# Sixteen-word gaps ahead of the two halves of the experts' gathered tokens

## The reference, cut to what matters

```python
def moe_swiglu(h, router, w_gate, w_up, w_down):
    top_v, top_i = lax.top_k(logits, TOP_K)
    ...
    for e in range(N_EXPERTS):
        y_e = swiglu(t, w_gate[e], w_up[e], w_down[e])   # (silu(t @ gate) * (t @ up)) @ down
        out = out + gates[:, e:e + 1] * y_e
```

## The kernel before

| begins at | tensors |
|---|---|
| 0 | `mslot0` to `mslot2`, `mix_parts` (over them), `consts`, `res`, the used start in `mixer_lows`, `x_pair` (byte 212736) and its second half (220928) |
| 64 | `weights_hi`, `weights_lo` (from byte 134720 on, 8192 each), `x_parts`, `hidden_hi`, `hidden_lo`, `mslot3` and `mslot3_parts`, `xn_hi`, `xn_lo`, `xT`, `one_hot`, `scratch` and `scratch_parts` (134720) |

## Time and profile before

### The profile page before, as it was taken

One profiled execution on the slowest core, in us unless ns is written; L12 is line 12 of the kernel. 1 busy time (PEld: TensorE's weight loads), 2 busy tenths in 40 slices (PEclk: granted clock), 3 DMA queues, 4 the chain that ended last, 5 costly groups with the idle time before them and its releaser, 6 DMA issues.

```text
span 2403.7 us, 34175 instructions
## 1 busy us (share of the span) xinstructions
PE 2382.4 (99%) x12542; PEld 2017.0 (84%) x12542; DVE 1872.4 (78%) x1961; ACT 1438.0 (60%) x1474; POOL 14.2 (1%) x34
## 2 busy tenths in 40 slices
PE   8999999999999999999999999999999999999998
PEld 7788899888888888888888888888788888897887
DVE  7767786678888888888888898677966676688666
ACT  6645455567777777777777776555254454544444
POOL 1000000000000000000000010000000000000000
PEclk9999999999999999999999999999999999999999
DMA  8375143459999999999999996853355566533653
GB/s 301 116 251 177 68 147 130 146 207 376 380 377 348 374 379 378 348 377 377 377 348 373 381 395 246 278 177 123 132 193 175 194 227 230 176 126 123 200 191 125
DMA packets 315952, 603.73 MB, mean 251 GB/s; under 512 B 9120, under 2 KB 135200, under 8 KB 315552
## 3 DMA queue, kind: packets, MB, share of 16 engines
q1 hardware_dynamic: 314160, 592.70, 69.1%
q10 hardware_dynamic: 1136, 7.87, 0.8%
q0 software_dynamic: 576, 2.10, 0.2%
HBM read 597.91 MB, written 8.91 MB: 252 GB/s over the span
## 4 chain that ended last, share of the span: by engine, by line
PE 94%; DVE 2%; ACT 1%; DMA 1%; DVEq 1%; issue 0%; SPq 0%; ACTq 0%
PE bank L205 20%; PE bank L206 20%; PE bank L207 19%; PE bank L1218 17%; PE bank L1222 9%; PE bank L3513 1%; PE bank L2955 1%; PE bank L3440 1%; PE bank L2230 1%; PE bank L2240 1%; DMA mslot<-in_e_w_in 1%; PE bank L2930 1%; PE bank L1714 1%; PE bank L1058 0%; PE bank L2149 0%; PE bank L2249 0%
## 5 line engine op out<-in xcount | busy, mean ns | idle before, releaser
L3205 DVE TENSOR_TENSOR weights_lo<-mslot,weights_hi 128x2048 fp32r<-128x2048 f32 x336 | 767.5, 2291 | 117.5 <-ACT weights_hi L3098 116.5
L3098 ACT ACTIVATE weights_hi<-mslot 128x2048 fp32r<-128x2048 f32 x336 | 644.0, 1919 | 217.4 <-PE bank L207 214.2
L1370 DVE TENSOR_TENSOR weights_lo<-scratch,weights_hi 128x2048 fp32r<-128x2048 f32 x165 | 377.2, 2289 | 166.3 <-ACT weights_hi L1363 166.2
L1218 PE MATMUL bank<-x_parts,weights_hi 128*128 128x512 f32 x1760 | 441.2, 392 | 1.8 <-DVE x_parts L921 1.8
L1218 PEld LDWEIGHTS bank<-x_parts,weights_hi 128*128 128x128 f32 x1760 | 319.4, 189 | 63.8 <-DVE x_parts L921 2.4
L205 PE MATMUL bank<-weights_hi,x_pair 128*128 128x512 f32 x896 | 356.9, 398 | 0.2 <-issue 0.2
L206 PE MATMUL bank<-weights_lo,x_pair 128*128 128x512 f32 x896 | 351.4, 392 | 0.0
L207 PE MATMUL bank<-weights_hi,x_pair 128*128 128x512 f32 x896 | 349.9, 391 | 0.0
L1363 ACT ACTIVATE weights_hi<-scratch 128x2048 fp32r<-128x2048 f32 x165 | 315.3, 1914 | 49.3 <-PE bank L207 49.0
L205 PE MATMUL bank<-weights_hi,hidden_hi 128*128 128x512 f32 x808 | 315.9, 391 | 0.0
L206 PE MATMUL bank<-weights_lo,hidden_hi 128*128 128x512 f32 x808 | 315.2, 390 | 0.0
(11 more groups left out here) (561 smaller groups left out, 2735.0 us busy)
## 6 DMA issues: line engine op xcount, KB each, us to landing
mslot<-in_o_moe_w_gate SPq DMA_DIRECT2D x112, 1024.0 KB, 6.8
mslot<-in_o_moe_w_up SPq DMA_DIRECT2D x112, 1024.0 KB, 6.8
mslot<-in_o_moe_w_down SPq DMA_DIRECT2D x112, 1024.0 KB, 6.9
scratch<-in_ffn_w_gate SPq DMA_DIRECT2D x44, 1024.0 KB, 5.2
scratch<-in_ffn_w_up SPq DMA_DIRECT2D x44, 1024.0 KB, 5.1
scratch<-in_ffn_w_down SPq DMA_DIRECT2D x44, 1024.0 KB, 5.0
mslot<-in_o_w_in SPq DMA_DIRECT2D x7, 2048.0 KB, 10.8
scratch<-in_e_ffn_w_gate SPq DMA_DIRECT2D x11, 1024.0 KB, 5.2
```

Of the source, the lines that this page charges most:

```text
L1218: pe.matmul(m.ps[bank + j][:, :], hi[:, k, cols(j)], both, start=(k == 0), stop=False)
L1370: dve.tensor_tensor(m.wlo[to][:, :], m.fslot[i], m.whi[to][:, :], ALU.subtract).then_inc(m.sig["f_lo"], 1)
L3098: act.activation(m.whi[(place + half) % PLACES][:, :], r.slot[slot + half], ACT.Copy).then_inc(s["r_hi"], 1)
L3205: dve.tensor_tensor(m.wlo[i][:, :], r.slot[slot + half], m.whi[i][:, :], ALU.subtract).then_inc(s["r_lo"], 1)
```

## The change

A tensor `phase3` of 16 words (64 bytes) is placed ahead of `x_pair`, and `x_pair` gets 16 words more. Its first half (`xg[0]`, the high part) then begins at byte 212800, 64 modulo 128, and the second (`xg[1]`, the low part), with another gap of 16 words before it, at byte 221056, 0 modulo 128. `m.xg` is a list of two tiles in place of one tile with an axis of two. In `odd_out_piece` the high part of the first half of block 9 was a slice of `x_pair` at word 2000; it is now written as a slice of `scratch_parts` at word 21504, which is byte 220736 like the slice before.

```diff
--- before.py
+++ after.py
@@ -48,6 +48,8 @@
 NE, FE = 8, 3584
 FC = 512
 NC = FE // FC
+
+PHASE = 16
 
 DA, DB, DC = 384, 256, 384
 AT = DA // P
@@ -190,7 +192,9 @@
     with nc.sbuf_tensor("mixer_lows", [P, f0 + 3 * PIECE - 6 * PIECE - KT * 2 * SEQ - 2 * HALF], F32R) as lows:
         m.c_low = [cut(lows, f0 - 6 * PIECE - KT * 2 * SEQ - 2 * HALF + i * KT * DC, KT, DC) for i in range(2)]
     sb("scratch_rest", f0 + PIECE - 6 * PIECE - KT * 2 * SEQ - 2 * HALF)
-    m.xg = cut(sb("x_pair", 2 * PIECE, F32R), 0, 2, KT, 2 * P)
+    sb("phase3", PHASE)
+    xg = sb("x_pair", 2 * PIECE + PHASE, F32R)
+    m.xg = [cut(xg, i * (PIECE + PHASE), KT, 2 * P) for i in range(2)]
     return m
 
 
@@ -496,7 +500,7 @@
     ks = slice(half * KT // 2, (half + 1) * KT // 2)
     wide = lambda t: t.rearrange("p (k n) -> p k n", n=HALF)
     if b == 9:
-        hi = m.xg.rearrange("p i k t -> p (i k t)")[:, PIECE - 48:2 * PIECE - 48] if half == 0 else \
+        hi = m.scr_parts(21504, PIECE) if half == 0 else \
             m.x2.rearrange("p k i t -> p (k i t)")[:, 0:PIECE]
         low = m.b_low
     else:
@@ -2790,7 +2794,7 @@
     flat = lambda t: t.rearrange("p k t -> p (k t)")
     x2 = m.x2.rearrange("p k i t -> p (k i t)")
     r.yh, r.yl = (x2[:, (2 + i) * KT * P:(3 + i) * KT * P] for i in range(2))
-    r.xg = [m.xg[:, i] for i in range(2)]
+    r.xg = m.xg
     xT = flat(m.xT)
     r.silu, r.h = xT[:, 0:FC], xT[:, FC:2 * FC]
     r.oh = m.oh.rearrange("p (t s) -> p t s", t=NT)
```

## The result

| | before | after |
|---|---|---|
| median of 21 runs, us | 2406.18 | 2409.65 |
| lowest run, us | 2405.57 | 2409.23 |
| span of the profiled execution, us | 2403.7 | 2407.8 |

The ratio is 1.0015, with a 95% interval of 1.0008 to 1.0021: 3.5 us slower, certain in its sign and under the 0.2% (4.8 us) that the prediction took as its bound. The forecast was 2411.4. One of the 21 runs of after took 2962.15 us at a mean granted clock of 0.752; the ratio leaves it out.

What follows compares the result with a forecast made beforehand. PE's sequence of matmuls in the expert stage was taken as the bound. 896 triplets x 6.3 ns = +5.6 us on 2405.8 gave 2411.4 us; range 2400.8 to 2414.3, the likeliest case's own 2409.5 to 2414.3.

Steps and rivals of the forecast that it cites:

- What bounds the stage: In the experts, PE is busy 950.00 of 950 us, so the stage lasts as long as PE's own sequence of matmuls.
- No other cost: No instruction, wait or byte of traffic is added; only matmul spacing in the experts' gate and up products changes.
- 693.3 per triplet: Experts' gate and up: three matmuls (alike, alike, different in place from the weights) take 693.3 ns, against 687 before.
- a passage that never ends: On `x_pair`, each alike/different change costs some 27 ns over about five matmuls; triplets change again before three are done.
- The sum, 896 x 6.3 = 5.6 us: Experts' gate and up products: 896 triplets of three matmuls, each 6.3 ns longer, all on the path, +5.6 us.
- the mechanism's lower bound: Least slowdown from mixed places in the experts' triplets, 896 x 4.4 ns = +3.9 us; the upper bound was +8.3 us.
- 24 steps in 5.55 where now 5.50: Timeline sign on `x_pair` in the experts: 24 matmul steps take 5.55 us after, where 5.50 passes without waits before.
- 27 ns x 56: Products on `hidden` behind the up product: their passage cost of 27 ns, 56 times, stays, within 1.5 us either way.
- Modulo 128: Experts' matmuls: whether stationary and moving operand begin alike modulo 128 bytes sets the spacing, 226.5 ns alike, 229.0 different.
- rival 2: Experts' gate and up: the high half decides and PE falls into 226.7 ns steps, -6.3 us, 2399.5 us; chance 0.13.
- Rival 1: Experts' gate and up: each product has its own price, prices add to 682.3 ns per triplet, -4.2 us; chance 0.13.
- Rival 3: The change doesn't act; the spacing of `x_pair` comes from something else, time stays at 2405.8 us; chance 0.12.

Runs made afterwards that it cites:

- e4: Against after, same places, but each half of a gate or up product does eight products with the high half, then four with the low: 2410.59 us.
- e6: Against after, both halves of `x_pair` placed at 192 modulo 256 bytes, the weights being at 64: 2415.75 us.
- e1: Against after, the low half of `x_pair` also placed at 64 modulo 256 bytes, so both halves lie like the weights: 2401.39 us.
- e3: Against after, high half of `x_pair` back at 0 as in before, low half at 128 modulo 256 bytes: 2412.24 us.
- e8: Against after, high half of `x_pair` kept at 64, low half placed at 192 modulo 256 bytes: 2410.74 us.
- e12: Against after, both halves of `x_pair` placed at 48 modulo 256 bytes, 16 bytes below the weights: 2402.7 us.
- e5: Against after, both halves of `x_pair` placed at 128 modulo 256 bytes, 64 above the weights: 2415.78 us.
- e11: Against after, both halves of `x_pair` placed at 32 modulo 256 bytes, 32 below the weights: 2415.33 us.
- e2: Against after, the places of `x_pair` mirrored, high half at 0 and low half at 64 modulo 256 bytes: 2407.67 us.
- e9: Against after, both halves of `x_pair` at 64, and low weights of the FFN's gate and up products at 128 and 0 modulo 256: 2399.64 us.

## Why the prediction was right or wrong

- *What bounds the stage*: right. PE is busy throughout in both kernels. In the ten further kernels that move `x_pair` alone or reorder its products, the time moved by -4.6 to +9.6 us, and the 112 groups of 24 account for it to within 0.5 us, but for e4 and e6, where the groups on `hidden` add 1.1 and 1.5. DVE, ACT and DMA followed even e1's shorter stage.
- *No other cost; the difference wholly between 510 and 1465 us; `hidden` and the FFN unchanged*: right, to 0.1 us (970 to 974 us, 2734.7 to 2735.9 ns, 928.7 to 928.8 us).
- *693.3 per triplet*: the rows of two alike and one different were the right ones to take it from; that a value picked between 692 and 694 came out to 0.1 ns is luck. The reason, a passage that never ends, isn't borne out. What came is a settled repeat of three, of the very kind that the forecast said would not be there, and e4 gets the same sum with a quarter of the passages. The passage of some 27 ns exists (28 in e4), but four of them in twelve matmuls don't cost four times as much. "Medians over 392 in at least two lines" was wrong with it: one line is over (397), another is at 392.
- *The sum, 896 x 6.3 = 5.6 us*: this is the term that was mis-sized. It measured 3.6 us by the groups and 3.5 by the medians. That is under the +3.9 that the prediction gave as the mechanism's lower bound. It held a time over +0.2% (0.48) likelier than one between that and no change by this mechanism (0.14), and the less likely of the two came. The step that failed is to price all 896 triplets at the settled step and to let the edges stay. "24 steps in 5.55 where now 5.50" was +50 ns; the mean group gave +32. The forecast had a passage of five steps in its own rows, and a group has only 24, so the edges are a large part of it. Before pays 61 ns per group at its two edges, after 41. The exit was named as a cost that stays (27 ns x 56), but the entries, 112 of them, were not summed at all.
- *Modulo 128*: wrong, by e3 (+6.2 us, where nothing was to change) and e6 (+9.5, where it should have been as fast as e1). The rows of before could not show it. All of them with 512 columns lay at distances 0 and -64 modulo 256; the prediction's remark that the low half goes "to an odd line of 128" where "no row of before has a stationary operand" was the right doubt, weighed in rival 2 only.
- *Rival 1, each product has its own price*: in the forecast's form (a gain of 4.2 us) it is refuted by after itself. With the distance modulo 256 it is still refuted: after and e8 settle at 693.3 where prices would add up to 686.7.
- *Rival 2, the high half decides*: refuted by after. The rhythm that it promised exists, but only once the low half is alike too (e1).
- *Rival 3, no effect*: refuted: operands' places alone moved the kernel from 2401.4 to 2415.8 us. The rule of the Trainium skill cited in the prediction ("SBUF — State Buffer", section "Who interferes with whom") has two parts. That PE's two read ports are independent isn't borne out, if it means that the places of the two operands don't bear on each other: with a stationary operand at 64, the step is 226.7 ns with the moving one at 64 and 229.0 with it at 128. That PE never waits on anyone is said there of other engines, and no run here bears on that.

What stays open: why mixed places cost more than their parts (693.3 against 686.7), and why operands at the same places can keep either of two rhythms (e3, e6, e12). That the settled sums are 680, 686.7, 693.3 and 700, always 6.7 ns apart, but for 685 in e12 and 697.3 in e6, is a fact of the traces and not an explanation. Moving the weights instead of `x_pair` was not tried, nor distances under 16 bytes, nor whether places beyond 256 bytes count.

## What to carry to other kernels

Where PE is busy without a gap, read the distance from start to start in the timeline and compare it between products of one shape: if they differ, look at where stationary and moving operand begin, modulo 256 bytes at the least, and put both halves at the moving operand's place (here -4.6 us for a gap of 16 words; moving only the high half there cost +3.5). Price a rhythm over the mean group with its edges, not at the settled step, and don't take a period or a mechanism for settled when all rows at hand are two cases of it; one kernel with a shift of 128 bytes would have told. The place is to be tried, not reasoned: 16 bytes off cost 0.9 to 1.3 us, 32 bytes off some 13.5.

## What the runs showed of the hardware that was not expected

- Float32r matmuls of 512 columns with a weight load each, at full clock, start 226.7, 228.3, 229, 232.4 or 233.3 ns apart, by where the stationary operand lies against the moving one modulo 256 bytes; sign counts (-64: 229, +64: 233.3).
- They fall into repeats of between 2 and 12 matmuls (2 in e5, 3 in before and after, 4 in e11, 6 in e2, 7 in e6, 12 in e3 and e4) and stay there to the end of the group; what ran before a group goes with which repeat it takes (e3: 687 or 700 per triplet with operands at the same places).
- Alike products behind different ones take some 28 ns more than behind alike ones, spread over about six matmuls (e4: 1842 against 1813 ns for eight).
- At 256 columns the cheaper place is another: all alike 119 to 120 ns, the low weights at 128 and 0 some 118 in the FFN (e9).
- The order of the products within a group changed the repeat but not its mean (e4: 693.3).
